# One chip step of a hybrid encoder trunk: the sample's search keys are computed in the mixer of block 1, and in the later mixers the first branch sum runs right behind the scores

## The chip, the cores and the metric

The kernel runs on 1 core of one Trainium2 chip. Its metric is the device time of one execution in microseconds (us). The kernel before takes 4076.27 us (median of 3 runs, 4074.62 to 4079.49).

A core has a matrix engine (TensorE, PE in the profile), a vector engine (VectorE, DVE), a scalar engine (ScalarE, ACT), a general engine (GpSimd, POOL) and a queue engine (SyncE, SP). Each runs its own list of instructions in order and waits on semaphores. Matrix products go to PSUM, 8 banks of 128 x 512 f32. 16 DMA engines carry all transfers, whichever engine issues them.

## The reference, cut to what matters

One layer over 1024 prompt rows and 128 sample rows (9 blocks of 128 rows, block 0 is the sample), D = 1024, all in f32.

```
def reference(x_prompt, x_sample, ...):
    for xp:                                             # the same for xs, with caches
        z = rmsnorm(x) @ w_in                           # 1024 -> 5888 columns
        qa, ka, va, qb, kb, vb, rg, ga, gb = split(z)
        oa = swa(qa, ka, va, sinks)                     # 8 heads of 64, 192 keys, softmax
        ob = retention(qb, kb, vb)                      # 4 heads, state 128 x 256
        ob = groupnorm(ob) * silu(rg)
        mix = sigmoid(ga) * (oa @ w_branch_a) + sigmoid(gb) * (ob @ w_branch_b)
        x = x + mix @ w_out
        h2 = rmsnorm(x)
        q = h2 @ w_q                                    # 8 heads x 256
        s1, s2 = q_lo @ sub_k1.T, q_hi @ sub_k2.T       # 128 + 128 scores a head
        idx, gate = top16(top16(s1) + top16(s2)), softmax
        act = gelu(h2 . expert_u[idx])                  # 128 experts a row, of 16384
        x = x + sum(gate * act * expert_v[idx])
        y = rmsnorm(x)
```

## The kernel before, in words

The program is a row of stages, each an `nc.Block()`: all engines finish a stage before the next begins. Times are those of the profiled execution.

1. Projection of blocks 0 and 1 (to 180 us).
2. The mixer of block 0, the sample (to 344 us).
3. **The mixer of block 1** (344 to 469 us): `pe_block`, `act_block`, `dve_block` (L617 to L749) with `merge=False`, then the merge of its own block: gated transposes, `pe_branches`, `pe_mix_transposes`, `pe_output`. SP loads the query matrix `w_q` (8 MB into `rows64`) once the second branch sum is there (`load_queries`, L817). GpSimd copies parts 46 to 61 of a joined table `uv_d` of u and v rows in DRAM (`pool_table`, L145 and L146).
4. **The search stage** (469 to 1194 us). PE computes the search keys of block 0 and then of block 1 (`pe_keys`: 8 transposes of `H` at L930, 64 passes against `w_q` at L935, transposes of `Q` at L939, scores at L943), with ACT copying between; then it projects blocks 2 to 8: 112 products (L1260), whose results ACT takes out of 8 PSUM banks in turn (L1289). VectorE searches block 0 (20 `PARTS` of `dve_keys`) and then takes gathered expert rows one by one: 256 for block 0, with the search of block 1 in between, and 96 for block 1 (`dve_experts`, `dve_experts_ahead`). GpSimd waits for `xg` and the first two tiles of `w_in`, copies table parts 62 to 87, and then issues the 352 gathers (L992), at most 16 ahead of VectorE, since the ring of 16 rows lies over `w_q`. ACT applies the gelus for VectorE (L968) at fixed places among its 112 copies (`gelu_at`: at copies 9, 19, ... 79, then 89, 96, 102), so each side can wait for the other.
5. **The later mixers** (1194 to about 1672 us), blocks 2 to 8. From block 3 on, the merge of block b-1 is folded into the mixer of block b (`merge=True`). VectorE has 8 places (`dve_point(v, blk, 0..7)`) where it handles the rest of block 1's expert rows: an even place takes 3 value rows (L1513, from block 3 on), an odd place 3 dot rows (L1496). GpSimd issues each group of 3 gathers when the group before it of the same kind has been used. SP loads the next block's rows and copies four table parts a block.
6. The search of block 2 and the end of block 8's merge (to 1793 us), then the expert stage of blocks 2 to 8 (to 4110 us), a loop of gathers of joined rows, which the change does not touch.

In a later mixer PE's order is: 13 transposes (L308), attention scores (L625), retention scores in bank 4 (L347), gated transposes (L315), a wait for `atm`, the first branch sum (L323) and the second (L328), 16 transposes of the probabilities (L639), transposes of the mix (L334), values (L647), retention (L652, L653), output product (L341), state product (L661). VectorE makes `atm` (L725) only after it has read the attention scores (L722, L723), and it reads those after the gate product (L432), the biases (L436) and place 0.

## Time and profile before

| | us |
|---|---|
| median of 3 runs | 4076.27 |
| the profiled execution | 4112.39 |
| its span | 4110.5 |
| PE, DVE, POOL, ACT busy in it | 3301.0, 2452.1, 1758.0, 1096.7 |
| mixer of block 1 (SP's first issue to SP's first issue of the next stage) | 343.6 to 469.2 |
| search stage | 469.2 to 1193.9 |
| later mixers, the search of block 2, the end of block 8's merge | 1193.9 to 1793.4 |
| expert stage of blocks 2 to 8 | 1793.4 to 4110.5 |

The busy times are those of the whole span; they mix stages with different limits. The page's chain of waits covers only the last stage, because it does not reach back over the barrier between stages; each stage before it has to be read by its own rows. A released wait is given in brackets behind a row: idle time and who ended it. "remote" and "issue" are idle times that the profile puts down to nothing on this core's engines.

### The profile page before, as it was taken

How to read it: one execution, taken by the hardware profiler on the slowest of the kernel's cores; microseconds unless marked ns; L12 is line 12 of the kernel's file. 1: busy time of each engine (PE TensorE's matmuls, PEld its weight loads, DVE VectorE, ACT ScalarE, POOL GpSimd, SP SyncE). 2: the span in 40 equal slices, each digit the busy share in tenths (PEclk: the TensorE clock that was granted, in tenths of full speed). 3: DMA queues.
4: the chain of work that ended last, by engine and by line, in shares of the span. 5: the costliest groups of instructions: out<-in, count | busy, mean ns of one | idle time of the engine just before them, and what ended most of it. 6: DMA issues, size and time to landing. Idle time of an engine off the chain costs nothing.

```text
span 4110.5 us, 32129 instructions
## 1 busy us (share of the span) xinstructions
PE 3301.0 (80%) x8957; PEld 1632.7 (40%) x8957; DVE 2452.1 (60%) x4977; ACT 1096.7 (27%) x2938; POOL 1758.0 (43%) x1588
## 2 busy tenths in 40 slices
PE   8775597999966888859779779878878978977776
PEld 5453254555644454424224224323333423422222
DVE  0122068995766777555854864774684585485444
ACT  2102010011113333223333233333333333333322
POOL 1020147774743333124454444444444444445553
PEclk9886897999987898979999999999999999999999
DMA  9898999998998888899999999999999999999998
GB/s 351 295 301 311 340 314 400 386 390 343 373 381 334 317 307 306 305 359 421 421 421 416 416 418 400 421 413 410 419 409 409 422 405 411 419 407 423 422 422 353
DMA packets 303298, 1560.95 MB, mean 380 GB/s; under 512 B 31248, under 2 KB 59152, under 8 KB 179856
## 3 DMA queue, kind: packets, MB, share of 16 engines
q0 software_dynamic: 228096, 1300.34, 79.3%
q1 hardware_dynamic: 60448, 237.77, 15.4%
q10 hardware_dynamic: 14592, 21.10, 1.4%
q8 instruction: 51, 0.84, 0.1%
q14 instruction: 111, 0.91, 0.1%
HBM read 1515.44 MB, written 179.04 MB: 412 GB/s over the span
## 4 chain that ended last, share of the span: by engine, by line
DMA 26%; PE 18%; issue 6%; DVE 4%; ACT 1%; POOL 1%; POOLq 0%; ACTq 0%; DVEq 0%
DMA ring<-uv_d,IXD_p 26%; PE ps L1838 15%; PE ps L1810 3%; DVE ring L1937 2%; ACT dg L1881 1%; POOL ring L2043 1%; ACT GE_p L1875 0%; DVE BP_p L1007 0%; DVE CA_p L1012 0%; DVE BV_p L1002 0%; PE ps L1827 0%; DVE CA_p L1419 0%; DVE DOT_p L1937 0%; DVE II_p L1359 0%; DVE ACC L1918 0%
## 5 line engine op out<-in xcount | busy, mean ns | idle before, releaser
L1838 PE MATMUL ps<-ring,dg 128*128 128x512 f32 x3584 | 1704.1, 614 | 456.5 <-ACT dg L1881 428.2
L2043 POOL DMA_INDIRECT ring<-uv_d,IXD_p x896 | 1081.3, 1207 | 1306.6 <-PE ps L1838 1050.1
L1937 DVE CUSTOM_DVE_ANT_0 ring<-ring,H 128x1024 f32<-128x1024 f32 x896 | 1094.6, 1224 | 888.5 <-DMA ring<-uv_d,IXD_p 866.0
L1838 PEld LDWEIGHTS ps<-ring,dg 128*128 128x128 f32 x3584 | 663.5, 194 | 1415.9 <-issue 717.7
L1260 PE MATMUL ps<-w,xg 128*128 128x368 f32 x1792 | 577.9, 482 | 43.8 <-issue 41.3
L1875 ACT ACTIVATE GE_p<-DOT_p 128x2 f32<-128x2 f32 x448 | 91.1, 203 | 1483.3 <-DVE DOT_p L1937 1483.3
L1260 PEld LDWEIGHTS ps<-w,xg 128*128 128x128 f32 x1792 | 345.6, 193 | 275.7 <-issue 70.2
L1881 ACT ACTIVATE dg<-gdi,GE_p 128x128 f32<-128x128 f32 x896 | 310.7, 394 | 48.3 <-ACT GE_p L1875 3.9
L1869 ACT ACTIVATE gdi<-ident,GD_p 128x128 f32<-128x128 f32 x896 | 303.2, 386 | 25.8 <-issue 19.4
L145 POOL DMA_DIRECT2D uv_d<-in_peer_u x88 | 45.7, 520 | 493.7 <-DMA uv_d<-in_peer_v 283.2
L1289 ACT ACTIVATE zo<-ps,rstd 128x368 f32<-128x368 f32 x112 | 62.6, 567 | 521.7 <-PE ps L1260 284.0
L1810 PE MATMUL ps<-rows,hT_p 128*128 128x512 f32 x384 | 197.0, 595 | 0.0
L1532 POOL DMA_INDIRECT rv<-in_peer_v,IXD x80 | 85.9, 1074 | 223.7 <-DVE AC L1513 207.2
L992 POOL DMA_INDIRECT rows<-in_peer_u,IXD_s x128 | 157.2, 1228 | 55.3 <-issue 43.0
L226 PE MATMUL ps<-w,xg 128*128 128x368 f32 x512 | 161.4, 479 | 13.9 <-DMA w<-in_w_in 13.9
L992 POOL DMA_INDIRECT rows<-in_peer_v,IXD_s x128 | 148.1, 1157 | 51.1 <-issue 38.1
L1124 DVE CUSTOM_DVE_ANT_0 rows<-rows,H_s 128x1024 f32<-128x1024 f32 x128 | 150.9, 1222 | 25.3 <-DMA rows<-in_peer_u,IXD_s 22.1
L1135 DVE SCALAR_TENSOR_TENSOR ACC_s<-rows,WG_s,ACC_s 128x1024 f32<-128x1024 f32 x126 | 155.5, 1293 | 9.4 <-issue 6.1
L1540 POOL DMA_INDIRECT ru<-in_peer_u,IXD x80 | 78.9, 986 | 133.7 <-DVE DOT L1496 95.0
L226 PEld LDWEIGHTS ps<-w,xg 128*128 128x128 f32 x512 | 98.7, 193 | 76.1 <-issue 16.4
L1513 DVE SCALAR_TENSOR_TENSOR AC<-rv,WG,AC 128x1024 f32<-128x1024 f32 x80 | 102.7, 1284 | 40.9 <-DMA rv<-in_peer_v,IXD 34.3
L1496 DVE CUSTOM_DVE_ANT_0 ru<-ru,H 128x1024 f32<-128x1024 f32 x80 | 95.9, 1222 | 38.2 <-DMA ru<-in_peer_u,IXD 34.6
(412 smaller groups left out, 2877.3 us busy)
## 6 DMA issues: line engine op xcount, KB each, us to landing
uv_d<-in_peer_u POOLq DMA_DIRECT2D x88, 512.0 KB, 5.2
uv_d<-in_peer_v POOLq DMA_DIRECT2D x88, 512.0 KB, 6.3
w<-in_w_in SPq DMA_DIRECT2D x8, 2944.0 KB
w<-in_w_in SPq DMA_DIRECT2D x16, 1472.0 KB
z_d<-zo ACTq DMA_DIRECT2D x16, 1288.0 KB
rows<-in_peer_w_q SPq DMA_DIRECT2D x20, 1024.0 KB
uv_d<-in_peer_u SPq DMA_DIRECT2D x40, 512.0 KB
uv_d<-in_peer_v SPq DMA_DIRECT2D x40, 512.0 KB
```

The costliest lines, as they stand in the source:

```text
L226: mm = T.matmul(ps[:, m % AB, 0:WC], xg0[:, k, b * P:(b + 1) * P], w0[:, p % 2, n % 2, k, :], start=(k == 0), stop=(k == KT - 1))
L992: gather = g.indirect_dma_start(ring[:, n % RING, :], None, t["peer_u"] if kind == "u" else t["peer_v"], bass.IndirectOffsetOnAxis(ap=inde ...
L1124: V.tensor_tensor_reduce(out=row, in0=row, in1=H2[:], scale=1.0, scalar=0.0, op0=ALU.mult, op1=ALU.add, accum_out=DOT[:, k:k + 1]).then_in ...
L1135: V.scalar_tensor_tensor(ACC[:, k % 2], row, WG[:, k:k + 1], ACC[:, k % 2], ALU.mult, ALU.add).then_inc(d["freed"], 1)
L1260: mm = T.matmul(ps[:, n % AB, 0:WC], xg[:, k, b * P:(b + 1) * P], w[:, tile % 2, k, :], start=(k == 0), stop=(k == KT - 1))
L1513: V.scalar_tensor_tensor(AC1[:], row, WG1[:, k % SET:k % SET + 1], AC1[:], ALU.mult, ALU.add).then_inc(d["accz"], 1)
L1810: mm = T.matmul(bank(2 + n), hT[:, k, :], wq[:, k, n * 512:(n + 1) * 512], start=(k == 0), stop=(k == KT - 1))
L1838: mm = T.matmul(bank(6 + n), dg[:, k % DR, :], ring[:, k % RS, D + n * 512:D + (n + 1) * 512], start=(k == 0), stop=(k == NK - 1))
L1869: S.activation(gdi[:, k % GR, :], ident[:], ACT.Copy, scale=GD[:, k:k + 1]).then_inc(e["gdi"], 1)
L1881: S.activation(dg[:, k % DR, :], gdi[:, k % GR, :], ACT.Copy, scale=GE[:, k:k + 1]).then_inc(e["diag"], 1)
L1937: V.tensor_tensor_reduce(out=row, in0=row, in1=H2[:], scale=1.0, scalar=0.0, op0=ALU.mult, op1=ALU.add, accum_out=DOT[:, k:k + 1]).then_in ...
L2043: g.indirect_dma_start(ring[:, n % RS, :], None, uv_d, bass.IndirectOffsetOnAxis(ap=IXD[:, n:n + 1], axis=0)).then_inc(s_ring[n % RS], 16)
```

## The change

Three things are done.

**Keys of the sample.** `pe_keys` and `act_keys_first` are cut in two (`pe_keys_rows`, `act_keys_rows` hold the transposes of `H` and their copy). The buffers of the keys (`kt`, `H`, `hT`, `SC`, `Q`, `qT`) are made before the stage of block 1's mixer and live on into the search stage, so they need room there: small buffers (`mx` to `sdv`) move into spare columns of `rows64`, and the constant mask `alibi_c` into half of `zv`. The stage of block 1 now loads `H` and the key tables, and computes the keys of block 0 behind its own output product. In the search stage only block 1's keys are left ahead of the projection, and VectorE multiplies `xg` by the gains between parts 2 and 3 of the search of block 0 and not ahead of it.

**Order in the mixers.** `pe_branches` and `dve_merge` are cut in two. In `pe_block` the first branch sum comes right behind the attention scores, then the gated transposes, then the retention scores, now in bank 0 (so they wait until VectorE has read the attention scores), then the second branch sum, and the wait for `atm` behind it. ACT does the exponentials before it copies the gated transposes. VectorE reads the scores and does the maxima right behind the gate product; the copies and biases, `atm`, the sums of the probabilities come next, and places 0 and 1 only then.

**Places.** VectorE's order in a mixer is now: scores and maxima, copies, biases, `atm`, sums of the probabilities, places 0 and 1, the first product of the merge, place 2, the rest of the merge, places 3 and 4, the retention norm, places 5, 6 and 7, the residual. Before it was: copies, biases, place 0, scores, `atm`, maxima, place 1, sums, places 2 and 3, the merge, places 4 and 5, the retention norm, places 6 and 7, the residual.

No size of a table part, no gelu place and no load of the later stages is changed (TABLE_BS, TABLE_E, TABLE_S, `gelu_at`, `GELUS1_AT` are as before). In the diff the first pieces are of the mixers, then those of the stage of block 1, then those of the search stage.

```
 def pe_block(pe, blk, half, merge):
     ...
             mm.then_inc(s["scores"], 1)
             pe.wait_ge(s["stn"], blk)
-            pe_scores_b(pe, blk, 4)
-            if merge:
-                pe_gated_transposes(pe, blk - 1)
-            pe.wait_ge(s["atm"], blk + 1)
             if merge:
                 if blk == 3:
                     pe.wait_ge(s_wb, 16 * 7)
-                pe_branches(pe, blk - 1)
+                pe_first_branch(pe, blk - 1)
+                pe_gated_transposes(pe, blk - 1)
+            pe.wait_ge(s["sm_s"], blk + 1)
+            pe_scores_b(pe, blk, 0)
+            if merge:
+                pe_second_branch(pe, blk - 1)
+            pe.wait_ge(s["atm"], blk + 1)
             pe.wait_ge(s["prob"], blk + 1)
 def act_block(act, blk, half, merge):
     ...
+            act_exps(act, blk, 2 * P)
             if merge:
                 act_gated(act, blk - 1)
-            act_exps(act, blk, 2 * P)
 def dve_block(v, blk, half, merge):
     ...
             if merge:
                 dve_gate(v, blk - 1)
+            ...
+            V.scalar_tensor_tensor(Pr[:, :, P:], sc[:, :, P:], HD ** -0.5, alibi[:, :, P:], ALU.mult, ALU.add)
+            V.scalar_tensor_tensor(Pr[:, :, 0:P], sc[:, :, 0:P], HD ** -0.5, ...).then_inc(s["sm_s"], 1)
+            dve_softmax(v, blk, 2 * P, sink[:], step)
             wait_mixers(v, blk, half)
             ...
             if merge:
                 dve_biases(v, blk - 1)
-            dve_point(v, blk, 0)
-            ...
-            V.scalar_tensor_tensor(Pr[:, :, P:], sc[:, :, P:], HD ** -0.5, alibi[:, :, P:], ALU.mult, ALU.add)
-            V.scalar_tensor_tensor(Pr[:, :, 0:P], sc[:, :, 0:P], HD ** -0.5, ...).then_inc(s["sm_s"], 1)
             v.wait_ge(s["st"], blk + 1)
-            V.tensor_tensor(atm..., bank(4), intra..., ALU.mult).then_inc(s["atm"], 1)
-            dve_softmax(v, blk, 2 * P, sink[:], step)
-            dve_point(v, blk, 1)
+            V.tensor_tensor(atm..., bank(0), intra..., ALU.mult).then_inc(s["atm"], 1)
             dve_probs(v, blk, 2 * P, False)
-            for half_point in range(2, 4):
+            for half_point in range(2):
                 dve_point(v, blk, half_point)
             if merge:
                 dve_merge(v, blk - 1)
-            for half_point in range(4, 6):
+            dve_point(v, blk, 2)
+            if merge:
+                dve_merge_rest(v, blk - 1)
+            for half_point in range(3, 5):
                 dve_point(v, blk, half_point)
             ...
             dve_retention_norm(v, blk, 2, step)
-            for half_point in range(6, 8):
+            for half_point in range(5, 8):
                 dve_point(v, blk, half_point)
 ...
                 def _(sp):
                     ...
                     load_rows(sp, 1)
+                    sp.dma_start(H[:], rows(h2_d, 0)).then_inc(c["hld"], 16)
+                    load_keys_tables(sp)
                     load_branches(sp)
                 def _(pe):
                     ...
                     pe_mix_transposes(pe, 1)
+                    pe_keys_rows(pe, 0)
                     pe_output(pe, 1)
+                    pe.wait_ge(s_cw, 16 * (KT + 2))
+                    pe.wait_ge(s["x1"], 2)
+                    pe_keys(pe, 0)
                 def _(act):
+                    act.sem_inc(c["v1"], 1)
                     ...
                     act_mix(act, 1)
+                    act_keys_rows(act, 0)
                     act_square2(act, 1)
                     act_root2(act, 1)
+                    act_keys_first(act, 0)
+                    act_keys_second(act, 0)
 ...
                 def _(sp):
-                    sp.dma_start(H[:], rows(h2_d, 0)).then_inc(c["hld"], 16)
+                    sp.dma_start(H[:], rows(h2_d, 1)).then_inc(c["hld"], 16)
                     sp.dma_start(io[:], t["iota16"]).then_inc(s_cw, 16)
-                    load_keys_tables(sp)
                     ...
-                    sp.wait_ge(c["ht"], 1)
-                    sp.dma_start(H[:], rows(h2_d, 1)).then_inc(c["hld"], 16)
                 def _(pe):
-                    pe.wait_ge(s_cw, 16 * (KT + 3))
-                    pe_keys(pe, 0)
+                    pe_keys_rows(pe, 1)
                     pe_keys(pe, 1)
                 def _(v):
-                    v.wait_ge(s_xt, 16 + 16 * KT)
-                    for k in range(KT):
-                        V.tensor_scalar(xg[:, k, :], xg[:, k, :], gm[:, k:k + 1], None, ALU.mult).then_inc(s_xg, 1)
                     v.wait_ge(s_cw, 16 * (KT + 3))
                     v.wait_ge(d["nf"], 16)
                     step = Steps(v, s_vstep, STEPS_C)
                     for part in range(PARTS):
+                        if part == GAIN_AT:
+                            v.wait_ge(s_xt, 16 + 16 * KT)
+                            for k in range(KT):
+                                V.tensor_scalar(xg[:, k, :], ...).then_inc(s_xg, 1)
                         dve_keys(part, v, 0, step)
```

PE's list around the keys, before: `H_s` are the rows h2 of a block, `rows` at L935 is `w_q`; the two branch rows are the ends of a stage.

```order
74 L328 MATMUL ps<-rows,yT_e 128x512 x16
75 L334 MATMUL ps<-ident,gates_e 128x128 x8
76 L341 MATMUL ps<-wo_e,yT_e 128x512 x16
77 L843 UNCONDITIONAL_BRANCH
78 L1245 UNCONDITIONAL_BRANCH
79 L930 MATMUL ps<-ident,H_s 128x128 x8
80 L935 MATMUL ps<-rows,hT_s 128x512 x32
81 L939 MATMUL ps<-ident,Q_s 128x128 x16
82 L943 MATMUL ps<-kt_s,qT_s 128x128 x16
83 L930 MATMUL ps<-ident,H_s 128x128 x8
84 L935 MATMUL ps<-rows,hT_s 128x512 x32
```

The same place of the change (its line numbers are shifted: L881 to L897 are the keys).

```order
74 L331 MATMUL ps<-rows,yT_e 128x512 x16
75 L337 MATMUL ps<-ident,gates_e 128x128 x8
76 L881 MATMUL ps<-ident,H_s 128x128 x8
77 L344 MATMUL ps<-wo_e,yT_e 128x512 x16
78 L889 MATMUL ps<-rows,hT_s 128x512 x32
79 L893 MATMUL ps<-ident,Q_s 128x128 x16
80 L897 MATMUL ps<-kt_s,qT_s 128x128 x16
81 L1165 UNCONDITIONAL_BRANCH
82 L1285 UNCONDITIONAL_BRANCH
83 L881 MATMUL ps<-ident,H_s 128x128 x8
84 L889 MATMUL ps<-rows,hT_s 128x512 x32
```

The keys of block 0 have moved across the end of the stage; those of block 1 stay.

PE's list in a merged mixer, before: scores, retention scores, gated transposes, the two branch sums, transposes of the probabilities, of the mix.

```order
105 L625 MATMUL ps<-kaT,qaT_p 128x256 x8
106 L347 MATMUL ps<-qbT_p,kbT_p 128x128 x4
107 L315 MATMUL ps<-ident,gates_p 128x128 x8
108 L323 MATMUL ps<-rows,oaT_p 128x512 x8
109 L328 MATMUL ps<-rows,yT_p 128x512 x16
110 L639 MATMUL ps<-ident,Pr_p 128x128 x16
111 L334 MATMUL ps<-ident,gates_p 128x128 x8
```

The same place of the change.

```order
105 L632 MATMUL ps<-kaT,qaT_p 128x256 x8
106 L323 MATMUL ps<-rows,oaT_p 128x512 x8
107 L315 MATMUL ps<-ident,gates_p 128x128 x8
108 L350 MATMUL ps<-qbT_p,kbT_p 128x128 x4
109 L331 MATMUL ps<-rows,yT_p 128x512 x16
110 L648 MATMUL ps<-ident,Pr_p 128x128 x16
111 L337 MATMUL ps<-ident,gates_p 128x128 x8
```

The first branch sum (L323) has moved ahead of the two short groups.

VectorE's list in the mixer of block 4, from the gate product to the probabilities, before (`AC<-rv` are value rows, `ru,DOT` dot rows).

```order
635 L432 TENSOR_TENSOR gates_p<-gates_p,yn_p 128x1024
636 L708 COPY va<-rows 128x128
637 L710 TENSOR_SCALAR kdec_p<-rows,outd_p 128x128 x4
638 L436 TENSOR_TENSOR gates_p<-gates_p,bg_p 128x2048
639 L1504 TENSOR_TENSOR WG<-GE,GD 128x12
640 L1513 SCALAR_TENSOR_TENSOR AC<-rv,WG,AC 128x1024 x3
641 L722 SCALAR_TENSOR_TENSOR Pr_p<-ps,rows 128x8x128
642 L723 SCALAR_TENSOR_TENSOR Pr_p<-ps,rows 128x8x128
643 L725 TENSOR_TENSOR atm_p<-ps,intra_p 128x512
644 L392 TENSOR_REDUCE mx_p<-Pr_p 128x8
```

The same place of the change.

```order
635 L435 TENSOR_TENSOR gates_p<-gates_p,yn_p 128x1024
636 L720 SCALAR_TENSOR_TENSOR Pr_p<-ps,rows 128x8x128
637 L721 SCALAR_TENSOR_TENSOR Pr_p<-ps,rows 128x8x128
638 L395 TENSOR_REDUCE mx_p<-Pr_p 128x8
639 L397 TENSOR_TENSOR mx_p<-mx_p,sink_p 128x8
640 L399 TENSOR_SCALAR ngm_p<-mx_p 128x8
641 L400 TENSOR_TENSOR es_p<-sink_p,mx_p 128x8
642 L724 COPY va<-rows 128x128
643 L726 TENSOR_SCALAR kdec_p<-rows,outd_p 128x128 x4
644 L439 TENSOR_TENSOR gates_p<-gates_p,bg_p 128x2048
645 L733 TENSOR_TENSOR atm_p<-ps,intra_p 128x512
```

The reading of the scores has moved ahead of the copies, the biases and the three value rows.

## Rows read from the trace of the kernel before

**Rows 1.** Stretches: us, each engine's busy time, PE clock, DMA share, GB/s

```profile
469.20:1193.90 724.70, 653.94 (x2032) 386.45 (x2032) 541.92 (x975) 87.47 (x146) 447.85 (x404) 0.94 0.96 366
1000.00:1100.00 100.00, 100.00 (x325) 61.40 (x324) 66.05 (x92) 14.26 (x27) 55.98 (x44) 1.00 0.82 306
1399.70:1468.20 68.50, 55.27 (x205) 31.91 (x205) 53.00 (x83) 25.41 (x46) 25.14 (x24) 0.93 0.86 314
```

**Rows 2.** SP timeline at the ends of the stages

```profile
446.69 0.34 SPq L301 DMA_DIRECT2D h_d<-yT_e  x1
469.19 0.34 SPq L1217 DMA_DIRECT2D H_s<-h_d  x1
...
1193.91 0.32 SPq L760 DMA_DIRECT2D rows<-z_d  x1
```

**Rows 3.** DMA issues from 440 to 469 us: KB each, us to landing

```profile
h_d<-yT_e SPq DMA_DIRECT2D x1, 512.0 KB, 14.7
```

**Rows 4.** PE timeline, output product and keys: start, us, line, tiles, [idle before]

```profile
425.49 15.70 PE L341 MATMUL ps<-wo_e,yT_e 128*128 128x512 f32 x32 [1.11 <-ACT yT_e L373]
474.41 1.97 PE L930 MATMUL ps<-ident,H_s 128*128 128x128 f32 x8 [33.22 <-DMA kt_s<-in_sub_k2t]
477.49 29.24 PE L935 MATMUL ps<-rows,hT_s 128*128 128x512 f32 x64 [1.11 <-ACT hT_s L948]
...
517.74 1.60 PE L930 MATMUL ps<-ident,H_s 128*128 128x128 f32 x8 [2.06 <-ACT SC_s L959]
...
562.94 57.46 PE L1260 MATMUL ps<-w,xg 128*128 128x368 f32 x185 [1.97 <-ACT SC_s L959]
```

**Rows 5.** DMA queues from 420.7 us (issue of `w_q`) to 455.0 us: packets, MB, share

```profile
q1 hardware_dynamic: 1204, 8.61, 62.1%
```

**Rows 6.** POOL timeline: first table part of the search stage, first gather

```profile
491.74 0.52 POOL L145 DMA_DIRECT2D uv_d<-in_peer_u  x1 [28.46 <-DMA w<-in_w_in]
...
587.51 1.00 POOL L992 DMA_INDIRECT rows<-in_peer_u,IXD_s  x1 [2.92 <-issue]
```

**Rows 7.** VectorE timeline, search stage

```profile
585.25 0.29 DVE L1077 TENSOR_REDUCE GS_s<-GT_s 128x8 f32<-128x128 f32 x1 [13.62 <-ACT GT_s L963]
...
1019.87 0.18 DVE L1113 TENSOR_TENSOR WG_s<-GE_s,GD_s 128x16 f32<-128x16 f32 x1 [29.61 <-ACT GE_s L968]
```

**Rows 8.** Waits from 563 us to 1194 us: who for whom, us, times, longest

```profile
DVE WG_s L1113 <- ACT GE_s L968: 54.5, 5, 29.6
```

**Rows 9.** PE timeline, mixer of block 5 (and block 4's merge)

```profile
1399.68 2.96 PE L625 MATMUL ps<-kaT,qaT_p 64*128 64x256 f32 x16 [2.90 <-ACT kbT_p L670]
...
1414.02 9.71 PE L323 MATMUL ps<-rows,oaT_p 128*128 128x512 f32 x16 [9.07 <-DVE atm_p L725]
1423.56 13.90 PE L328 MATMUL ps<-rows,yT_p 128*128 128x512 f32 x32
...
1440.03 1.09 PE L334 MATMUL ps<-ident,gates_p 128*128 128x128 f32 x8 [0.83 <-DVE gates_p L445]
```

**Rows 10.** VectorE timeline, the same mixer

```profile
1402.58 1.22 DVE L432 TENSOR_TENSOR gates_p<-gates_p,yn_p 128x1024 f32<-128x1024 f32 x1
...
1411.01 1.22 DVE L722 SCALAR_TENSOR_TENSOR Pr_p<-ps,rows 128x1024 f32<-128x1024 f32 x1
...
1437.49 1.22 DVE L443 TENSOR_TENSOR gates_p<-gates_p,ps 128x1024 f32<-128x1024 f32 x1 [5.73 <-PE ps L328]
...
1456.92 2.71 DVE L1513 SCALAR_TENSOR_TENSOR AC<-rv,WG,AC 128x1024 f32<-128x1024 f32 x2 [1.95 <-DMA rv<-in_peer_v,IXD]
...
1463.25 1.22 DVE L450 TENSOR_TENSOR X_p<-X_p,ps 128x1024 f32<-128x1024 f32 x1
```

**Rows 11.** ACT timeline, the same mixer

```profile
1408.26 1.02 ACT L369 ACTIVATE yT_p<-ps 128x1024 f32<-128x1024 f32 x1 [7.12 <-DMA h_d<-yT_p]
...
1416.66 0.21 ACT L352 ACTIVATE es_p<-es_p 128x8 f32<-128x8 f32 x1 [6.08 <-DVE es_p L397]
...
1420.62 0.18 ACT L354 ACTIVATION_READ_ACCUMULATOR Pr_p<-Pr_p,ngm_p 128x1 f32 x1
```

**Rows 12.** Waits of PE from 1331 to 1605 us, four merged mixers

```profile
PE ps L323 <- DVE atm_p L725: 29.7, 4, 9.1
```

More of the change, by code:

```diff
@@ L706, in dve_block @@
                 dve_gate(v, blk - 1)
+            if blk <= 2:
+                v.wait_ge(s_mask, 16 * 4 + 48 * blk)
+            v.wait_ge(s["scores"], blk + 1)
+            sc = ps[:, 0:4, :].rearrange("p b (h n) -> p (b h) n", h=2)
+            V.scalar_tensor_tensor(Pr[:, :, P:], sc[:, :, P:], HD ** -0.5, alibi[:, :, P:], ALU.mult, ALU.add)
+            V.scalar_tensor_tensor(Pr[:, :, 0:P], sc[:, :, 0:P], HD ** -0.5, alibi_c[:] if blk == 1 else alibi[:, :, 0:P], ALU.mult, ALU.add).then_inc(s["sm_s"], 1)
+            dve_softmax(v, blk, 2 * P, sink[:], step)
             wait_mixers(v, blk, half)
@@ L715, in dve_block @@
                 dve_biases(v, blk - 1)
-            dve_point(v, blk, 0)
-            if blk <= 2:
-                v.wait_ge(s_mask, 16 * 4 + 48 * blk)
-            v.wait_ge(s["scores"], blk + 1)
-            sc = ps[:, 0:4, :].rearrange("p b (h n) -> p (b h) n", h=2)
-            V.scalar_tensor_tensor(Pr[:, :, P:], sc[:, :, P:], HD ** -0.5, alibi[:, :, P:], ALU.mult, ALU.add)
-            V.scalar_tensor_tensor(Pr[:, :, 0:P], sc[:, :, 0:P], HD ** -0.5, alibi_c[:] if blk == 1 else alibi[:, :, 0:P], ALU.mult, ALU.add).then_inc(s["sm_s"], 1)
             v.wait_ge(s["st"], blk + 1)
-            V.tensor_tensor(atm[:].rearrange("p h n -> p (h n)"), bank(4), intra[:].rearrange("p h n -> p (h n)"), ALU.mult).then_inc(s["atm"], 1)
-            dve_softmax(v, blk, 2 * P, sink[:], step)
-            dve_point(v, blk, 1)
+            V.tensor_tensor(atm[:].rearrange("p h n -> p (h n)"), bank(0), intra[:].rearrange("p h n -> p (h n)"), ALU.mult).then_inc(s["atm"], 1)
             dve_probs(v, blk, 2 * P, False)
-            for half_point in range(2, 4):
+            for half_point in range(2):
                 dve_point(v, blk, half_point)
@@ L1187, in trunk_kernel @@
+        q_.close()
         with ExitStack() as m:
-            kt, H, hT, SC, CA, DOT, GE, WG, nf, m4 = search_buffers(m, "_s")
+            ACC = sb(m, "ACC_s", [P, 2, D])
+            X1 = sb(m, "X1_s", [P, D])
+            H2 = sb(m, "H2_s", [P, D])
+            CA, DOT, GE, WG, nf, m4 = search_buffers(m, "_s")
             VV, II, IF, BV, BP, AU, AF, I12, IX, GT, GS = list_buffers(m, "_s")
@@ L1265, in _ @@
                 def _(act):
-                    act.sem_inc(c["v1"], 1)
                     act.sem_inc(s_zact, AB)
-                    for blk in range(2):
-                        act_keys_first(act, blk)
-                        act_keys_second(act, blk)
+                    act_keys_rows(act, 1)
+                    act_keys_first(act, 1)
+                    act_keys_second(act, 1)
                     for n in range(WT * PB):
@@ L1327, in _ @@
                     pool_gathers(g, 1, ORDER1, IXD1)
+        early.close()
         PG, PTS = 3, 4
```

168 lines of the change are left out of this document (94 added, 74 removed).

## The prediction, written before the result was known

> **What bounds the kernel now.** The page's chain of waits reaches back only through the last stage, so each earlier stage is read by its own rows. The last stage has nothing of the change in it; a gain or loss ahead of it passes to the end one for one. I read the stretches first [rows 1]: the reader is to see that in the search stage the DMA share is 0.96 and no other engine is as full as that (PE 654 of 725 us, VectorE 542), and that in a later mixer nothing is full: PE 55.3 of 68.5 us, VectorE 53.0, DMA 0.86. A full resource sets the first, a chain that goes back and forth between engines the second. Then the ends of the stages [rows 2]: 469.19 and 1193.91 us. Then the timelines around the two places of the change.
>
> The stage of block 1: PE's output product runs 425.49 to 441.19 [rows 4], then PE has no work until 474.41. The 469.19 comes from the store of h2: issued 446.69, 14.7 us to landing, 461.4 [rows 2, 3]. In the search stage the keys of block 0 take from 474.41 to 517.74, those of block 1 from there to 562.94, when the projection starts [rows 4]. GpSimd waits for `w`, starts the table at 491.74, 22.5 us into the stage, and gathers from 587.51, 118.3 us into it [rows 6]. VectorE had its list at about the same time, 585.25, after a 13.62 us wait for ACT [rows 7]: the two sides now meet. Later VectorE waits 54.5 us for gelus, 29.61 of it at 1019.87 [rows 7, 8], and there the DMA share is 0.82 [rows 1].
>
> The mixer of block 5: PE waits 9.07 us for `atm` ahead of the first branch sum [rows 9]; four blocks have 29.7 us of this [rows 12]. The cause is on VectorE: it takes the gate product at 1402.58 and reads the scores only at 1411.01, although PE had written them by 1402.64 [rows 9, 10]. Then the second branch sum is late for VectorE (5.73 us wait), and the mix is transposed at 1440.03 [rows 9, 10]. But the block ends with the residual at 1463.25, behind six expert rows, one of which waited 1.95 us for its gather [rows 10].
>
> **The change, part one: keys of block 0.** Removed from the search stage: 517.74 − 474.41 = 43.3 us of PE ahead of the projection. Added to the stage before: the transposes of `H` run ahead of the output product, so from the passes on it is 517.74 − 477.49 = 40.25 us [rows 4]. They start when `w_q` is there: its eight tiles are 8.39 MB and the queue had moved 8.61 MB by 455.0 [rows 5], so 455.0 at the latest, and PE is free since 441.2. The stage ends at 455.0 + 40.25 = 495.3 and not at 469.2: **26.1 us later**. Block 1's keys then need the load of `H`, 474.41 − 469.19 = 5.2 us, and 562.94 − 517.74 = 45.2 us: projection from 545.7, 17.2 us earlier. So PE and ACT gain 17 and GpSimd loses 26, since its table starts 22.5 us after the stage and its gathers 118.3: 613.6. VectorE's search took 585.25 − 517.74 = 67.5 us; it can start when the gains of the norm have landed, at an estimate 25 us into the stage like `w`, so its list is there by about 590, with the product of `xg` in it a little more. It no longer sets the gathers; the table does. That is what is late next.
>
> How much of the 26.1 is kept at the stage's end? Two bounds. If the gather phase keeps its length, all: the stage ends at 1220.0, +26.1. If only the work of the DMA engines counts, the stage has 0.96 × 724.7 = 695.7 us of it, and at a share of 1.00 it ends at 495.3 + 695.7 = 1191.0, −2.9. Between: the 100 us around the gelu wait run at 0.82, all else at (695.7 − 82) / 624.7 = 0.982. The gelus stand at fixed copies of the projection, which is now 17 us earlier while the gathers are 26 us later, 43 us in all, and the longest wait is 29.61; so the dip goes, and with 0.982 throughout the stage takes 708 us and ends near 1203, less the loads of the keys that have left it. **Taken: +8**, range −3 to +26.
>
> The DMA share that decides here is that of one pool: 0.96 with GpSimd, SP and ACT all issuing [rows 1]. The Trainium skill, "DMA: Bandwidth & Descriptors", section "Issuing engines are not separate DMA queues", says that transfers of the scalar, sync and gpsimd engines run on the same 16 engines and interleave. By that rule the total is what counts, −3; by GpSimd's own chain (late table, late gathers) it is +26. The rule also speaks against the change: the earlier loads and stores of the projection will slow the table.
>
> Edits at nothing: the load of `H` and the key tables in block 1's stage (issued far ahead of the 26 us in which the DMA engines now have nothing to do); the small buffers and the mask in other places; ACT's copy of the transposes of `H`, beside the output product. If that copy delayed ACT's square and root, the h2 store would land later, but it has 495.3 − 461.4 = 34 us of cover.
>
> **Part two: order in the later mixers.** For block 5, counted from the scores at 1399.68. VectorE ends the gate product at 1403.8 and reads the scores then, 7.2 us earlier than at 1411.01 [rows 10]. From that reading to the exponentials it was 1416.66 − 1411.01 = 5.65 us [rows 11], now without `atm` in between about 5.0: 1408.8. The exponentials take 1416.66 to 1420.8, 4.1 us, then ACT copies the gated transposes, 1.02 us [rows 11]: 1414.0. On PE: scores to 1402.6, first branch sum 7 to 9.7 us, and the two short groups 2.3: 1412 to 1414.6. So the second branch sum starts at about 1414.5 and not at 1423.56, **9 us earlier**, and so does the mix: 1431 and not 1440.03. VectorE needs until then: 1408.8, copies and biases 3.1, `atm` and sums 1, two places, a product, a place. Three value rows are 1.5 × 2.71 = 4.1 us, three dot rows 1463.25 − 1459.63 = 3.6 [rows 10]: 4.1 + 3.6 + 1.2 + 4.1, in all 1426. In time.
>
> Not all 9 us come out at the end. VectorE now has places 3 and 4 behind the merge (1438.6 with 3.6 + 4.1 from 1431), the norm with PE's retention (it was 9 us later), 1439 to about 1443.6, and then three places, 3.6 + 4.1 + 3.6 = 11.3 us: 1454.9. Moving place 5 behind the norm also moves its gathers: the dot rows of place 7 are only asked for when place 5 is done, at 1447.2, and place 6 covers just 4.1 us of their latency. I count a stall of 2 to 5 us there, from the waits of 1.95 [rows 10] and of GpSimd's way. The residual is then at 1457 to 1460 and not at 1463.25, and what follows is as before: 3.5 to 6 us a block; taken 4.5. Blocks 4 to 7: four times 4.5 = 18; block 3, which has the shorter wait (its share of the 9.07 kind is small), 1.5; block 8, which has no such dot rows at the end, 5; block 2, which has no merge and whose VectorE waits for gathers anyway, −1 for a burst that is now three places long. **Together −23.5**, bounds −6 (a gain of 1 a block) and −45 (9 in five blocks: the whole wait). The DMA share would rise from 0.86 to 0.86 × 68.5 / 64 = 0.92, not full.
>
> **Sum.** +8 − 23.5 = −15.5 us on the profiled execution (4112.39, span 4110.5), which is 36 us above the median of the runs, 4076.27. I take the difference over unchanged: 4076.3 − 15.5 = 4060.8, say 4061.
>
> **Rivals.** *The shift is kept (slower).* Place: GpSimd at the start of the search stage. Its table waits for `w`, its gathers for the table, and 352 gathers behind it are paced by a DMA pool that is as full as before. Price: +26.1, and if the mixers then give only 1 to 2 us a block, −8, the sum is +18: 4094. It decides as soon as what is kept is more than the mixers give back. For it: share 0.96 and hardly any slack in 725 us [rows 1]. Against: the dip at 1000 to 1100 [rows 1, 8].
>
> *The mixers are held by VectorE and the gathers (no change).* The three places behind the norm cost 7 us of waits where there were 2 and 3; a block gains 1 to 2 us, −8 in all, against +8: 4076. For it: expert rows already wait for their gathers when the queue holds other loads [rows 10]. Against: VectorE is busy only 53.0 of 68.5 us [rows 1].
>
> *Both go well.* Waits for gelus vanish, the gather phase shortens by all of the 26 (−3), and the mixers give 6 us a block, −32: −35, 4041. For it: 54.5 us of gelu waits [rows 8] and 29.7 of `atm` waits [rows 12]. Against: the DMA work stays.
>
> **How the numbers follow.** Forecast (−6 to −26 us) 0.43; both well 0.16; no change 0.19; slower 0.22. A measurement of this kernel tells some 0.2% (8 us) from none. Below −8: 0.40 of the forecast and the 0.16 of the good case, 0.56; within 8: 0.20; above: 0.24. Range 4034 to 4090: from the good case with a little more on the mixers to the slower one short of its full price. The likeliest case's own range is 4050 to 4070.
>
> **What would show it.** Right: SP's first issue of the search stage near 495; PE's passes against `w_q` starting near 455 and the projection near 546; GpSimd's first gather near 614 and no gelu wait over 10 us; stage end 1195 to 1210; `atm` waits of PE gone, first branch sum right behind the scores, residual to residual 63 to 65 us; and in its place VectorE waiting for `ru` ahead of the last dot rows. Wrong: a stage end at 1215 or more (the shift is kept), or below 1190 (PE or the gelus had set it, not the DMA); a period still at 67 or more (the gathers set it); a second branch sum that starts later than 16 us behind the scores (ACT's exponentials hold it).

## The result, and the profile after

The changed kernel takes 4141.5 us (median of 4 runs, 4135.8 to 4148.2); the kernel before, measured beside it, 4075.5. The ratio is 1.0161, 95% interval 1.0143 to 1.0178: 66 us slower. The forecast was 4061 us with a range of 4034 to 4090; its sign and its size were wrong.

The stretches of the changed kernel, in the columns of [rows 1]: the end of the stage of block 1's mixer, the search stage, and one period of a later mixer.

```profile
460.00:493.10 33.10, 27.79 (x100) 14.82 (x98) 0.00 (x0) 5.86 (x5) 2.78 (x6) 1.00 0.33 98
493.10:1180.80 687.70, 602.29 (x1912) 364.87 (x1912) 544.92 (x975) 76.41 (x140) 449.10 (x404) 0.93 1.00 385
1476.26:1551.31 75.05, 57.74 (x206) 33.77 (x206) 53.07 (x83) 25.44 (x46) 27.34 (x24) 0.86 0.81 286
```

The reader is to see three things. For 33 us the DMA engines are a third busy; then the search stage runs at a DMA share of 1.00; and this mixer period is 75 us (68.5 before) with the same VectorE work, 53 us, and a lower DMA share, 0.81 for 0.86. PE's rows at the keys answer to [rows 4]:

```profile
421.79 14.00 PE L344 MATMUL ps<-wo_e,yT_e 128*128 128x512 f32 x32 [0.24 <-ACT yT_e L376]
452.24 29.74 PE L889 MATMUL ps<-rows,hT_s 128*128 128x512 f32 x64 [16.45 <-DMA rows<-in_peer_w_q]
...
496.96 1.97 PE L881 MATMUL ps<-ident,H_s 128*128 128x128 f32 x8 [6.02 <-DMA H_s<-h_d]
...
540.70 39.68 PE L1299 MATMUL ps<-w,xg 128*128 128x368 f32 x122 [1.97 <-ACT SC_s L915]
```

SP's rows answer to [rows 2]:

```profile
493.11 0.34 SPq L1260 DMA_DIRECT2D H_s<-h_d  x1
...
1180.84 0.32 SPq L769 DMA_DIRECT2D rows<-z_d  x1
...
1816.89 0.34 SPq L2006 DMA_DIRECT2D H<-h_d  x1
```

Compared with the first trace of before, the search stage ends 13 us earlier (1180.8, 1193.9), the stretch from there to the expert stage is 636 and not 599.5 us, and the whole is 31 us longer. The medians of the plain runs say 66. A second profile of before (e1, below) shows where the rest lies.

The mixer of block 6, from its scores at 1476.26 (the rows of before show block 5), in the rows of PE that answer to [rows 9], then those of VectorE that answer to [rows 10]:

```profile
1476.26 5.65 PE L632 MATMUL ps<-kaT,qaT_p 64*128 64x256 f32 x16 [13.72 <-ACT kbT_p L679]
1481.84 9.76 PE L323 MATMUL ps<-rows,oaT_p 128*128 128x512 f32 x16
...
1493.58 14.00 PE L331 MATMUL ps<-rows,yT_p 128*128 128x512 f32 x32 [0.22 <-ACT yT_p L372]
...
1512.68 1.09 PE L337 MATMUL ps<-ident,gates_p 128*128 128x128 f32 x8 [3.35 <-DVE gates_p L450]
...
1551.31 5.65 PE L632 MATMUL ps<-kaT,qaT_p 64*128 64x256 f32 x16 [13.75 <-ACT kbT_p L679]
```

```profile
1481.95 1.22 DVE L720 SCALAR_TENSOR_TENSOR Pr_p<-ps,rows 128x1024 f32<-128x1024 f32 x1 [1.58 <-PE ps L632]
...
1494.64 2.69 DVE L1555 SCALAR_TENSOR_TENSOR AC<-rv,WG,AC 128x1024 f32<-128x1024 f32 x2
...
1507.26 1.28 DVE L1555 SCALAR_TENSOR_TENSOR AC<-rv,WG,AC 128x1024 f32<-128x1024 f32 x1 [1.55 <-DMA rv<-in_peer_v,IXD]
...
1521.86 1.28 DVE L1555 SCALAR_TENSOR_TENSOR AC<-rv,WG,AC 128x1024 f32<-128x1024 f32 x1 [4.50 <-DMA rv<-in_peer_v,IXD]
1524.93 1.28 DVE L1555 SCALAR_TENSOR_TENSOR AC<-rv,WG,AC 128x1024 f32<-128x1024 f32 x1 [1.78 <-DMA rv<-in_peer_v,IXD]
...
1546.36 1.22 DVE L455 TENSOR_TENSOR X_p<-X_p,ps 128x1024 f32<-128x1024 f32 x1
```

PE's new order works as meant: the wait for `atm` is gone, the first branch sum stands right behind the scores, the second starts 17.3 us behind the scores (23.9 before). But VectorE waits for value rows between the two parts of the merge and again ahead of the retention norm; the residual comes 70.1 us behind the scores (63.6 before), and PE then idles 13.75 us ahead of the next scores. Those take 5.65 us at a granted clock of 0.50 (1.2 GHz); in block 5 before they took 2.96 us at 1.00 (2.4 GHz). In blocks 3 to 8 of the changed kernel all scores take 5.65 us, before they took from 2.96 to 5.65. The loss lies behind the mix: its transposes come 36.4 us behind the scores, 4 us earlier than before (40.4), but from there to the residual it is 33.7 us and not 23.2. The waits of five merged blocks (1254.5 to 1624.5 us) in the changed kernel (total us, times, longest):

```profile
PE ps L632 <- ACT kbT_p L679: 50.4, 4, 13.9
DVE AC L1555 <- DMA rv<-in_peer_v,IXD: 47.6, 28, 5.1
...
DVE ru L1538 <- DMA ru<-in_peer_u,IXD: 17.1, 15, 1.7
```

The source is on GpSimd: the first gather of the block is issued 23.6 us behind the scores, after a long idle time, since place 0 only then has freed the buffers.

```profile
1499.88 1.14 POOL L1574 DMA_INDIRECT rv<-in_peer_v,IXD  x1 [24.26 <-DVE AC L1555]
```

### The profile page after: what moved, and what is told of

Same layout as the page of the kernel before. It is cut to its first block, busy times and chain, and to the rows that moved or that the text cites. A ratio compares the mean times of both kernels' runs of the same rounds, so it can differ in the third digit from the quotient of the medians.

```text
span 4141.9 us, 32143 instructions
## 1 busy us (share of the span) xinstructions
PE 3281.8 (79%) x8957; PEld 1631.7 (39%) x8957; DVE 2455.4 (59%) x4977; ACT 1092.2 (26%) x2938; POOL 1770.1 (43%) x1588
## 4 chain that ended last, share of the span: by engine, by line
DMA 25%; PE 18%; issue 7%; DVE 5%; ACT 1%; POOL 1%; POOLq 0%; ACTq 0%; DVEq 0%
DMA ring<-uv_d,IXD_p 25%; PE ps L1882 15%; PE ps L1854 3%; DVE ring L1981 2%; ACT dg L1925 1%; DVE BV_p L958 1%; POOL ring L2087 1%; DVE BP_p L963 0%; ACT GE_p L1919 0%; DVE CA_p L968 0%; DVE DOT_p L1981 0%; DVE CA_p L1460 0%; DVE ACC L1962 0%; PE ps L1871 0%; DVE VV_p L1395 0%
## 5 line engine op out<-in xcount | busy, mean ns | idle before, releaser
L1299 PE MATMUL ps<-w,xg 128*128 128x368 f32 x1792 | 564.8, 479 | 39.5 <-ACT zo L1327 37.5
L226 PE MATMUL ps<-w,xg 128*128 128x368 f32 x512 | 161.1, 478 | 14.2 <-DMA w<-in_w_in 14.2
L948 POOL DMA_INDIRECT rows<-in_peer_u,IXD_s x128 | 146.3, 1143 | 52.6 <-issue 37.7
L1582 POOL DMA_INDIRECT ru<-in_peer_u,IXD x80 | 88.0, 1100 | 129.8 <-DVE DOT L1538 98.0
```

Source lines behind the costliest of these rows:

```text
L226: mm = T.matmul(ps[:, m % AB, 0:WC], xg0[:, k, b * P:(b + 1) * P], w0[:, p % 2, n % 2, k, :], start=(k == 0), stop=(k == KT - 1))
L948: gather = g.indirect_dma_start(ring[:, n % RING, :], None, t["peer_u"] if kind == "u" else t["peer_v"], bass.IndirectOffsetOnAxis(ap=inde ...
L1299: mm = T.matmul(ps[:, n % AB, 0:WC], xg[:, k, b * P:(b + 1) * P], w[:, tile % 2, k, :], start=(k == 0), stop=(k == KT - 1))
```

## The experiments

**Both kernels again, and the two halves of the change.** e1 is the kernel before, unchanged. e2 keeps the moved keys and takes `pe_block`, `act_block` and `dve_block` of before; e3 is the kernel before with these three functions of the change. Theory and rival of each run are in its expectation.

> The kernel before, unchanged, to get a second profiled execution of it. The profiled execution that the prediction was read from took 4112.4 us, 36 us more than the median of its plain runs (4075.5), while that of the changed kernel took 4143.9 against a median of 4141.5. Theory A (the profiled execution of before was an unusual one): this profile comes near 4076 us, and the stage that is shorter in it by some 35 us is the one in which the comparison of the two traces misleads; I expect the search stage (724.7 us in the first profile, 690 here), because PE was starved for 22.8 us and VectorE waited 29.6 us for a gelu there. Rival B (profiling itself costs 36 us in this kernel): again 4110 to 4115 us. Ratio to the kernel before 1.000 either way.

> The changed kernel with the mixers' order and places of the kernel before: only the keys of the sample have moved. Theory (the whole loss is the later mixers): the stretch from the start of the later mixers to the expert stage takes 599 us as before, the search stage ends near 1181, 13 us earlier than in the first profile of before, total 4141.5 - 36.6 - 8 = about 4097 by plain runs if the plain runs of before have no shorter search stage, so 4097 or less. Rival (the shift of the stage's end is kept against ordinary runs of before, whose search stage is shorter than the profiled one): above 4076 by 15 to 26 us, 4091 to 4101.

> The kernel before with only the order and the places of the mixers changed (keys of the sample still in the search stage). Theory (places 0 and 1 behind the probabilities bunch the gathers in the last two thirds of a block): merged blocks take 73 to 75 us instead of 68.5, PE waits 9 to 14 us ahead of the scores, VectorE 40 us or more for rv in four blocks, total 4075 + 37 = 4112 (4105 to 4120). Rival (the slow mixers come from what the moved keys do to buffers or transfers): 68 us a block or less, 4055 to 4080.

Measured: e1 4076.9 us, ratio 0.9998 [0.9988, 1.0007]; e2 4099.4, ratio 1.0063 [1.0046, 1.0079]; e3 4115.2, ratio 1.0103 [1.0086, 1.0120]. Before stood at 4077.5. The halves cost 22 and 38 us, together 60 of the 66. So e2's theory, that the mixers are the whole loss, is wrong and its rival holds; e3's theory holds. The end of the stage of block 1 and the search stage, first in e1, then in e2:

```profile
455.00:473.60 18.60, 0.00 (x0) 0.00 (x0) 0.00 (x0) 0.00 (x0) 3.06 (x6) 0.50 0.80 255
473.60:1161.70 688.10, 630.47 (x2032) 381.16 (x2032) 545.00 (x975) 86.57 (x146) 450.44 (x404) 0.96 1.00 386
```

```profile
455.00:492.70 37.70, 32.36 (x110) 16.90 (x108) 0.00 (x0) 5.86 (x5) 3.65 (x8) 0.99 0.38 114
492.70:1180.30 687.60, 600.94 (x1912) 364.01 (x1912) 544.99 (x975) 76.58 (x140) 449.78 (x404) 0.93 0.99 385
```

The search stage takes 688.1 us with the keys of block 0 in it and 687.6 without, PE busy for 630 or 601 us, at a DMA share of 1.00 and 0.99: its length is that of its DMA work, not PE's. Idle DMA time ahead of it is 18.6 x 0.20 = 3.7 us in e1 and 37.7 x 0.62 = 23.4 in e2; the difference, 19.7, is the shift of the stage's start (492.7 - 473.6 = 19.1) and of its end (1180.3 - 1161.7 = 18.6). Next to nothing of it was given back. The execution from which the prediction was read had a search stage of 724.7 us. That of e1 took 4081.9 us in all and 688.1 in this stage, and e3, e12, e14 and e15, which also have both blocks' keys in it, took 687.9 to 691.0: theory A of e1 holds, and profiling does not cost 36 us.

**Filling the gap.** e5 is e2 with one number changed.

```
-TABLE_A, TABLE_BS, TABLE_E, TABLE_S, TABLE_P = 24, 46, 62, 88, 108
+TABLE_A, TABLE_BS, TABLE_E, TABLE_S, TABLE_P = 24, 46, 70, 88, 108
```

> The kernel with only the keys moved (4099.4 us), and TABLE_E = 70 for 62: eight table parts more are copied in the stage of block 1's mixer, where the DMA engines now stand idle, and 18 in the search stage for 26. Theory (the search stage is 688 us of DMA work with the keys in it or not, so the later start is kept in full, and the loss is the 25 us of idle DMA ahead of it): 8 x 3.57 us = 28.6 us less in the search stage, little or nothing more in the stage before; the stage end goes back from 1180 to 1155 (+-5), total 4073 to 4079. Rival (GpSimd's chain of gathers sets the stage, 352 gathers of 1.7 us each): the gathers start earlier by the same 28 us, so the total is the same 4075, but then the DMA share of the search stage falls below 0.97; if neither holds and PE or the gelus set the stage, the total stays at 4095 or more.

Measured: ratio 1.0007 [0.9983, 1.0031]; on this chip before itself took 4107.8 us, so only the ratio counts (e2: 1.0063). The runs of e5 spread from 4076.3 to 4134.1 us, and the profiled one is the fastest of them. Its two stages:

```profile
344.80:500.50 155.70, 98.01 (x325) 56.55 (x325) 23.90 (x46) 30.82 (x49) 24.52 (x48) 0.80 0.93 334
500.50:1161.70 661.20, 610.59 (x1912) 365.59 (x1912) 543.65 (x975) 80.44 (x140) 438.25 (x388) 0.95 1.00 388
```

Eight parts less make the search stage 26.4 us shorter and its DMA share stays 1.00, so GpSimd's chain is not the limit. The stage before ends 7.8 us later than in e2, and the search stage ends at 1161.9, where it ends in e1 (1161.6). e11 below, on another chip and in an execution at its median, shows the same: with `TABLE_E` = 70 its search stage is 662.2 us, with 62 it is 688.5 in e9 and 687.9 in e10 on that chip. The moved keys, with the gap filled, gain nothing that the ratio can show (it is good to some 10 us), and the traces show why: PE's 43 us were not on the path.

**Where the mixers lose: early places.** From here the period of a merged block is the mean over five (scores of block 3 to those of block 8): 67.2 us in e1, 67.4 in e2, 74.0 in the change, 72.8 in e3. e4 puts VectorE's places early in the changed order, e8 the same but place 0 a step later, behind the biases. `dve_block` in e4:

```
             dve_softmax(v, blk, 2 * P, sink[:], step)
+            dve_point(v, blk, 0)
             ...
             V.tensor_tensor(atm..., bank(0), intra..., ALU.mult).then_inc(s["atm"], 1)
+            dve_point(v, blk, 1)
             dve_probs(v, blk, 2 * P, False)
-            for half_point in range(2):
-                dve_point(v, blk, half_point)
+            dve_point(v, blk, 2)
             if merge:
                 dve_merge(v, blk - 1)
-            dve_point(v, blk, 2)
+            dve_point(v, blk, 3)
             ...
-            for half_point in range(3, 5):
+            for half_point in range(4, 6):
             ...
-            for half_point in range(5, 8):
+            for half_point in range(6, 8):
```

> The changed kernel with place 0 right behind the maxima, place 1 behind atm, place 2 behind the sums of the probabilities, place 3 behind the first product of the merge, 4 and 5 ahead of the retention norm, 6 and 7 behind it; PE's and ACT's order as in the change. Theory (late places are the loss, the order of PE is not): the waits for rv fall from 38.8 us in four blocks to 10 to 15, a block takes 64 to 68 us, the total falls by 5 x 8 = 40 us below the change's 4141.5: about 4100. Rival (PE's new order costs, since atm and the second branch sum now wait for ACT and PE): a block stays above 71 us, 4120 to 4140.

> As the run with early places (4116.7 us), but place 0 stands behind the biases instead of ahead of the copies. So the copies of VectorE end 4 us earlier, SP's burst (keys part and two table parts, which waits for them) is issued earlier than the gathers of place 2 and not with them, and ACT has its biases earlier. Theory (the 4.9 us wait of place 2 for rv and PE's 6.6 to 8.1 us wait for the mix come from that burst): periods from 70 to 67, total 4117 to 4100 to 4105. Rival (atm, the sums and with them the probabilities are what PE waits for): no better than 4117, since place 0 now delays atm by up to 1 us.

Measured: e4 4116.7 us, ratio 1.0103 [1.0086, 1.0120], period 69.7; e8 4129.0 us beside 4107.8 of before on its chip, ratio 1.0061 [1.0036, 1.0085], period 67.9. In e8 that is near the period of before, and its ratio is that of e2: the keys' 22 us. e4's theory was half right: its 4100 us and its 64 to 68 us a block were too low, but the 71 us of its rival were not reached either. One step of place 0 made up most of what was missing, as e8's theory had it.

**Table parts in the mixers.** e6 and e7 are e2 and the change with `TABLE_P` = 88 for 108.

> Control for the next run: the kernel with only the keys moved, TABLE_P = 88 for 108, so that SP copies none of the 20 table parts during the mixers of blocks 3 to 7 and all of them after the mixers. Only the periods of the merged blocks are read, not the total, which grows at the end of the mixers. Theory (places and order of the kernel before are bound by the chain PE-VectorE, little by gathers): periods from 68.0 to 65 to 67 us. Rival (bursts of table parts set them): under 64.

> The changed kernel with TABLE_P = 88 for 108: no table parts in the mixers of blocks 3 to 7. Theory (in the changed order the gathers are asked for late and close together, and what makes them late for VectorE is SP's burst of gates and table parts in front of them): periods fall from 74 to 66 to 68 us, the waits for rv and ru from 52 us in four blocks to under 20. Rival (the round trip of a gather, three rows a kind, is too long for the new spacing even on quiet queues): periods stay above 71 and the waits above 35.

Measured: 66.3 us a period in e6 (67.4 with the parts), 71.6 in e7 (74.0). The bursts cost 1.1 and 2.4 us a block; e6's theory holds, and for e7 the rival. Both took longer in all (4184 and 4202 us, one run each), in part because the 20 parts are then copied behind the mixers: from the end of the search stage to the expert stage it is 650.5 us in e6 and 598.2 in e2. The waits of e7 for rv and ru over five blocks are 38.6 + 15.1 = 53.7 us (64.7 in the change).

**Gathers taken away.** In `pool_values` and `pool_dots` of e9 and e10 (the same for `ru`; VectorE's dot rows read `H21` twice in place of `ru`):

```
                 for k in places(grp):
+                    if grp:
+                        g.dma_start(rv[:, k % PG, 0:16], t['peer_v'][0:P, 0:16]).then_inc(s_ring[11 + k % PG], 16)
+                        continue
                     g.indirect_dma_start(rv[:, k % PG, :], ...
```

> The changed kernel; in the later mixers all gathers but the first group of each kind are replaced by loads of 16 columns (64 bytes a row), and VectorE's dot rows take H21 twice in place of the row, so that the values are other ones but VectorE's work is the same. What is left out is the 512 KB of each of the other 154 gathers. Only the periods of the merged blocks are read. Theory (late gathers are what the new order costs; its chain of PE and VectorE is shorter): periods from 74 to 62 to 66 us, waits for rv and ru under 2 us a block. Rival (the new chain is itself longer, by scores and first branch sum at the lower clock, and the waits for gathers only fill it): periods stay at 70 or more.

> Control: the same replacement in the kernel with only the keys moved, whose mixers have the order and the places of before. Theory (17 us of waits for gathers in four blocks, partly hidden): periods from 68 to 65 to 67 us, and the wait of PE for atm, 7 us a block, stays. So without gathers the changed order is faster than this one by 1 to 3 us a block. Rival: it is not faster without gathers either.

The two stretches of five periods, the changed order (e9) and that of before (e10):

```profile
1247.70:1553.70 306.00, 283.76 (x1025) 166.58 (x1025) 261.36 (x413) 124.22 (x223) 63.47 (x120) 0.92 0.42 144
```

```profile
1237.00:1568.50 331.50, 281.96 (x1026) 165.21 (x1026) 261.85 (x413) 125.65 (x224) 63.45 (x120) 0.91 0.39 138
```

VectorE does the same 261 us in both. The changed order takes 61.2 us a block, that of before 66.3, with the wait for `atm` still there:

```profile
PE ps L323 <- DVE atm_p L733: 35.3, 5, 9.1
```

So the new order does shorten the chain of PE and VectorE, by 5.1 us a block. The gathers cost it 74.0 - 61.2 = 12.8 us a block, and the order of before, with the same gathers, only 67.4 - 66.3 = 1.1. So the theories of e9 and e10 hold, and the gain of the new chain is larger than the 1 to 3 us that e10 expected. These two kernels also take the bytes of the gathers away (DMA share 0.42 and 0.39), so by themselves they do not tell a gather that is asked for late from one that is slow. Moving the places, with all bytes kept, does (e8, e13). e9 took 4053 us and e10 4072 (one run each); both leave out most of the gathers of the later mixers.

**Attempts at a faster version.** e11 is e8 with `TABLE_E` = 70 and the second pair of table parts behind `load_rows`; e12 has the same mixers on the kernel before.

> A version that could beat both: place 0 behind the biases (as in the run before), eight table parts more in the stage of block 1's mixer (TABLE_E = 70), and the second pair of table parts of a block issued behind the stores at its end and not with the gates. Theory (VectorE's waits for ru, 6.4 us a block, come from the burst of gates and table parts at the mix): periods from 68 to 64 to 66, the stage ends as before, total 4060 to 4068, ratio 0.996 to 0.998. Rival (gathers wait for their own round trip; the burst only moves in front of the keys and values of the next block): 4075 or more.

> The same mixers as in the run with the combination, on the kernel before (keys of the sample in the search stage, TABLE_E = 62). Theory (search stage and stage of block 1 as before, only the mixers count): as the combination within 0.1%, 4060 to 4068. Rival (moving the keys and filling the gap gives something of its own, PE being free earlier): slower than the combination by 0.2% or more.

Measured: e11 4077.1 us, ratio 1.0009 [1.0000, 1.0018]; e12 4074.5, ratio 1.0003 [0.9994, 1.0012]. Before stood at 4072.9. Both periods are 67.6. The 4060 to 4068 us of both theories failed and the rival of e11 holds (4075 or more); e12 is within 0.1% of e11, as its theory said, so the moved keys with the gap filled gain nothing here either. The rows are waited for as before the move of the burst (51.8 us over five blocks, 49.0 in e8); that the burst is only in the way somewhere else is a reading, not tested by itself. In e11 PE waits for the mix:

```profile
PE ps L337 <- DVE gates_p L450: 31.4, 5, 8.3
DVE AC L1556 <- DMA rv<-in_peer_v,IXD: 26.3, 13, 5.3
DVE ru L1539 <- DMA ru<-in_peer_u,IXD: 25.5, 12, 5.2
```

**Which place.** e13 is the change with place 0 behind the biases. e14 and e15 stand on the kernel before; their VectorE order is biases, 0, `atm`, sums, 1, 2, the whole merge, 3, 4, then 5 ahead of the norm (e14) or behind it (e15).

> The changed kernel with place 0 alone moved: behind the biases and ahead of atm, while place 1 stays behind the sums of the probabilities, 2 between the parts of the merge and 5 behind the retention norm. Theory (the first gathers of a block are asked for when place 0 is done; that moment, 23 us behind the scores, is most of the loss): it comes 5 us earlier, periods from 74 to 69 to 71. Rival (place 5 behind the norm makes the stall, as the prediction had it): periods stay at 73 or more, with 4 us and more of waits for ru and rv behind the norm.

> On the kernel before (keys not moved, table as before): the changed order of PE and ACT; VectorE with place 0 behind the biases, atm, the sums of the probabilities, places 1 and 2, both parts of the merge, places 3, 4 and 5, the retention norm, places 6 and 7. So only one late group stands ahead of the merge. Theory (PE waits 4 to 8 us a block for the mix since place 3 and the late rows of place 2 stand ahead of it; without gathers the chain takes 61.3 us): the mix is ready 3 us earlier, periods 63 to 66, total 4050 to 4065. Rival (what is taken from in front of the merge comes back as waits ahead of the retention norm and the residual, since every group has the same round trip): periods 67 to 68, total 4070 to 4078.

> As the run before it, but place 5 stands behind the retention norm, as in the change. Theory (its rows land about when PE is done with the retention, so the norm is not held up by them): 0 to 2 us a block less than e14. Rival (the stall of the prediction: place 7's rows are asked for later and the residual waits): 2 to 3 us a block more than e14.

Measured: e13 4126.8 us (one run), period 71.1; e14 4093.3 us, ratio 1.0038 [1.0026, 1.0051], period 68.9; e15 4081.5 us, ratio 1.0014 [1.0005, 1.0022], period 68.3. Before stood at 4076.1. Place 0 alone is 2.9 of the 6.6 us that the change lost; the first gather of the block is then issued 19.0 us behind the scores and not 23.6. The theory of e14, 63 to 66 us, failed, and it was slower than even its rival had it (67 to 68): in e14 PE waits 0.8 us at most for the mix, but VectorE waits for three dot rows ahead of the norm in each block, and PE ahead of the scores instead. Its waits over five blocks:

```profile
PE ps L632 <- ACT kbT_p L679: 51.8, 5, 10.6
DVE ru L1506 <- DMA ru<-in_peer_u,IXD: 34.8, 15, 5.5
DVE AC L1523 <- DMA rv<-in_peer_v,IXD: 14.7, 7, 3.4
```

Over five blocks VectorE waits for rows 21.9 us in e2, 64.7 in the change, 49.0 in e8, 49.5 in e14, 40.7 in e15. Moving the places moves the wait; only the order of before, which spreads the places from 7 to 60 us of the block, keeps it small. The sum of the waits is not yet the loss: e8 has 49.0 us of them at 67.9 us a block and e2 21.9 at 67.4, which fits the shorter chain of the new order. No version with all its gathers beats the kernel before.

## Why the prediction was wrong, by its own steps

**The base.** The prediction saw that the profiled execution was 36 us above the median and carried the difference over unchanged. That failed first: all of it lay in the search stage (36.6 us more than in e1), on which the sum of part one was built. The gelu wait of 29.61 us and the dip to 0.82 at 1000 us, which were to vanish and so give back 18 of the 26 us, are not in an ordinary execution (e1: 688.1 us at 1.00, no wait of VectorE for a gelu). There was nothing to give back.

**Keys.** Nearly every step of the mechanism held: passes from 452.2 (forecast 455.0), stage end 493.1 (495.3), projection 540.7 (545.7), first gather 618.8 (613.6), no long gelu wait. The term "taken: +8" was mis-sized; measured are +19 at the stage's end and +22 in the total, inside its bounds of -3 to +26 and near its upper one. The first rival, "the shift is kept", named this, but put it down to GpSimd's own chain; it is the pool of DMA engines (e5). The Trainium skill, "DMA: Bandwidth & Descriptors", section "Issuing engines are not separate DMA queues", says that transfers of the scalar, sync and gpsimd engines run on the same 16 engines. The traces agree: the search stage is 688 us of DMA work in e1 and in e2. The bound of -3 held the stage's DMA work, 695.7 us, against the end of the long execution, 1193.9, in which the stage took 724.7 us. Against e1, where the stage is DMA work throughout, the same sum gives 495.3 + 688.1 - 1161.7 = +22. So the low bound was itself a product of the base.

**Mixers.** This is the step that failed in sign: forecast -23.5 us, measured +38 (e3). Its first half was right: the reading of the scores, the exponentials, the second branch sum earlier (17.3 us behind the scores; forecast 15, before 23.9). Without gathers the new chain is 5.1 us a block shorter (e9, e10), near the 4.5 that were taken. What failed is "In time": that VectorE has its places done as the branch sums end. The working added the places as 4.1 and 3.6 us of VectorE each, with one stall of 2 to 5 us at the end. In the mixer shown that stall is 4.3 us (four waits behind the norm), about as forecast. What was put at nothing is the waits for rows ahead of the norm: 2.7 us in place 2 and 6.3 in place 4, 9.0 in all. The rival "The mixers are held by VectorE and the gathers" named this wait, but even it counted a gain of 1 to 2 us a block; no case of the prediction had a loss here.

The prediction looked at place 5, which was moved behind the norm, and not at places 0 and 1. By its own sum place 0 starts some 13 us behind the scores; it started 18.4 us behind them (7.4 before), since the scores ran at the lower clock and `atm` waited 3.18 us for PE's retention scores. Its rows had long been in the buffers, GpSimd had nothing to issue for 24 us, and four groups of each kind had to be asked for and land in the rest of the block. e13 and e8 show it: place 0 alone is 2.9 us of the period, and with places 1, 2, 3 and 5 earlier too it is 6.1; how those four share the other 3.2 was not tested. Place 5 behind the norm does no harm: e15 is 0.6 us a block shorter than e14, and its ratio is lower, 1.0014 for 1.0038.

**Open.** The halves and e1 add up by their medians to 4137; the 4 us to 4141.5 are within the spread of the runs. The ratios give the halves 0.63 and 1.03%, which add up to a little more than the 1.61% of the whole. The expert stage, which no edit touches, is 2325.0 us in the changed kernel's profile, 2318.7 in e1's and 2315.8 to 2324.1 in the other runs'; the cause of these 6 us is not known.

Not known either is why the first profiled execution of before was long.

## What to carry to other kernels

A place where an engine uses a gathered row is also the moment at which the next gather is asked for; with one buffer set a kind, moving it later makes later uses wait even if the engine's own work is unchanged (2.9 us a block for place 0 alone), so list for each moved use when its successor is issued. Here 11 us of delay left GpSimd idle for 24. Before a gain is built on a wait or a dip in a profile, find the stage that holds the gap between the profiled execution and the median, and do not price anything from it; a second profile of the unchanged kernel finds it. In the one stage here that runs at a DMA share of 1.00, taking 43 us of PE out of it changed nothing, while 19 us of idle DMA time ahead of it and eight table parts fewer in it (26.4 us) came through in full.

## What was not expected of the hardware

One chip ran the unchanged kernel at 4107.8 us (19 runs, 4095 to 4122), another at 4077.5 (13 runs, 4070 to 4081), with the same program. The traces of three other kernels from the first of these chips show the longer search stage: 721.4 us in e6, 699.7 in e7 and 703.0 in e8, although their edits do not touch it and e2, with the same stage, took 687.6 elsewhere. So a long search stage like the 724.7 us of the first profile is seen again on that chip, and is not an effect of the change.

Idle time of PE ahead of the scores does not by itself tell their clock. After 13.72 us of it they took 5.65 us (clock 0.50) and after 2.90 us 2.96 (clock 1.00) [rows 9], but in e8 they took 5.65 us after only 2.58 us of idle time.
